# Expert gate and up rows laid over the partitions in pairs instead of in eights, in a one-core transformer and mixture-of-experts kernel

## The chip, the cores and the metric

The kernel runs on one NeuronCore of a Trainium2 chip. The metric is the device time of one execution in microseconds (us). TensorE multiplies, VectorE (DVE), ScalarE (ACT) and GpSimd (POOL) do the elementwise work, and SyncE (SP) issues every DMA of this kernel on one queue, which 16 DMA engines serve. All data is float32.

## The reference, cut to what matters

Two attention layers come first; they keep their code in this change. Behind the third, small attention layer stands a mixture of experts for 256 tokens of width 1024:

```python
# 32 experts, each token goes to a few of them
logits = h @ router_w                     # choose experts, weights wt[t, e]
for e in range(32):
    g = h @ gate_w[e]                     # gate_w[e]: 1024 x 512
    u = h @ up_w[e]                       # up_w[e]:   1024 x 512
    out += wt[:, e] * ((silu(g) * u) @ down_w[e])   # down_w[e]: 512 x 1024
```

gate_w, up_w and down_w are 2 MB (2,097,152 bytes) for each expert, 201 MB for all 32, and every expert's weights are read once. The contraction of g and u runs over the 1024 rows of gate_w[e] and up_w[e]; in which order the rows are taken doesn't matter, as long as the tokens' columns are taken in the same order.

## The kernel before

Weights travel through six buffers `ring0` to `ring5` of 128 partitions x 4096 elements (2 MB each), in the order of a list `chunks` in the front part (about 50 chunks of 2 KB runs for the most part), and by hand-written lines for the experts. `load_expert(j, e)` (L455) issues one load of 2 MB: j = 0, 1, 2 are gate, up and down of an even expert, 3, 4, 5 those of an odd one. Each load waits first until the ring buffer is free: `load_gathered` waits on the semaphore `g_gu` (a gate and up product is done) or `g_down` (a down product is done). The gate weights of experts 2, 6, 10, ... go to a seventh home, `probs` (`load_third_gate`, L461). Weights of experts 0 to 3 are loaded ahead, those of experts 2 and 3 partly in pieces into tiles that have become free (`load_third_up`, L466, into MOD; `load_fourth_up`, L471, into seven small homes; the gate of expert 3 into Y and hT). What is left when the first `g_gu` arrives is gate and up of experts 4 to 31 (28 + 28 loads) and down of experts 3 to 31 (29 loads, the last one in two halves): 85 loads of 2 MB.

The experts are taken in 8 quads of 4. A quad's tokens are gathered by matrix products: `gather(q, half)` (L2398) has a 128-column slice of the tokens' rows Y as the stationary operand and the selection matrix SEL (128 columns, 32 slots for each of four experts) as the moving one, so that XG gets the transposed tokens of four experts. Since a matmul in float32 is two instructions on TensorE, a half is 4 x 2 x 2 = 16 of them. Slice k of the contraction holds the rows 8p + k of the weights (p is the partition), so it is read as

```python
Y[:, t, 4 * half + k:D:KD]      # every eighth element, KD = 8
```

`gather_first(t)` (L2492) is the same for quad 0, taken in two steps t as soon as the tokens of 128 rows have chosen their experts. Ahead of the second step stand `place_second` (L2388, L2389, waits for the choice `mk` of the second 128 tokens) and one residual product (L2330). `gate_up(q, s)` (L2413) computes gate and up of one expert in 64 instructions of 32 stationary columns and 256 moving ones; `turn_hidden` (L2443) turns the hidden rows, with the stationary operand `HID[:, j:256:2]`, every second element; `down` (L2461) is the down product, `add_outputs` (L2478) adds four experts' outputs to the residual in PSUM.

TensorE's order inside a quad is written out by hand: for s = 0 to 3 gate_up, then for s = 0 the outputs of the quad before, for s = 1 and 2 one half of the gather of the next quad, then turn_hidden and down. The gather runs 14 times as a half (quads 1 to 7) and twice as gather_first. ACT copies the gathered tokens from PSUM (L917 for the first quad's first half), DVE the second half (L1762).

Before the quads SP, TensorE, DVE and ACT each read a flag (`crowd`, L1759) and branch: with at most 32 tokens for each expert they take the quads, and otherwise a dense path, which the data of this case doesn't take.

Of the kernel before, what the change touches and what calls it, by code (L numbers as in the profile page):

```python
# [8 lines left out]
P = 128  # L9
D = 1024  # L10
SEQ = 256
NT = SEQ // P
KD = D // P
# [7 lines left out]
FC = 4  # L21
# [66 lines left out]
def build(nc, x, ab_w, ab_out_w, cd_w, cmp_w1, cmp_w2, uq_w, ukv_w, cd_out_w, ada_w, ada_b, in_w, pool_mt, pool_w,  # L88
# [4 lines left out]
    with ctx:  # L93
        def sb(name, shape, dt=F32):
            return ctx.enter_context(nc.sbuf_tensor(name, shape, dt))
# [24 lines left out]
        def upto(name, n):  # L120

            return sem(name), before_stage.get(name, 0) + n

        def sem(name):
            name = stage_of.get(name, name)
            if name not in made:
                made[name] = ctx.enter_context(nc.semaphore("s_" + name))
            return made[name]


        ring = [sb(f"ring{i}", [P, SLOT]) for i in range(SLOTS)]
        X = sb("X", [P, NT, D])
        hT = sb("hT", [P, KD, SEQ])
        Y = sb("Y", [P, NT, AB_N])
        MOD = sb("MOD", [P, 6, D])
        QT = sb("QT", [P, 16, SEQ])
        probs = sb("probs", [P, SLOT])
        PB = probs[:, 0:2048].rearrange("p (a n) -> p a n", a=2)
        PTB = probs[:, 2048:4096].rearrange("p (a b n) -> p a b n", a=2, b=2)
        C = sb("C", [P, CO["cos64"][0] + 1024])  # L140
# [26 lines left out]
        bank = [banks[:, i, :] for i in range(8)]  # L167
# [6 lines left out]
        chunk0 = sb("chunk0", [P, 512])  # L174


        def const(name, rows=P):
            a, n = CO[name]
            return C[0:rows, a:a + n]
# [5 lines left out]
        ident = const("ident")  # L185
# [50 lines left out]
        def spare(a):  # L236
            return Y[:, 0, 2048 + a:2304 + a].rearrange("p (t n) -> p t n", t=NT)

        SEL, SW, SWT = spare(0), spare(256), spare(512)
# [4 lines left out]
        def rows(w, k):  # L244
            return w.rearrange("(p k) n -> p k n", k=k)
# [24 lines left out]
        half, first = KD // 2 * AB_WIDTHS[0], rows(ab_w, KD)[:, :, 0:AB_WIDTHS[0]]  # L270
# [49 lines left out]
        def eslot(j):  # L320

            return (E0 + j) % SLOTS

        hT_flat = hT[:, :, :].rearrange("p k n -> p (k n)")
# [61 lines left out]
        def gathered_landed(eng, q, s, j):  # L386
# [15 lines left out]
            if (e, j) in ahead:  # L402
# [2 lines left out]
            eng.wait_ge(*upto(f"slot{slot}", loads_of[slot] + 16 * (e // 2 + 1)))  # L405

        dead, late = CO["cos64"][0], KD + D
        up3_homes = [(0, 1, chunk0[:, :]), (1, 2, C[:, dead:dead + 1024]), (3, 1, Y[:, 1, 2048:2560]),
                     (4, 1, SMB[:, late:late + 512]), (5, 1, latent[:, 0:512]), (6, 1, soft[:, :]), (7, 1, tmp[:, :])]

        block = ctx.enter_context(nc.Block())
# [9 lines left out]
        def _(sp):  # L421
# [7 lines left out]
            off, n, k, src = first_rows  # L429
            sp.dma_start(ring[0][:, off:off + n].rearrange("p (k n) -> p k n", k=k), src).then_inc(sem("ld_first"), 16)  # L430
            for i, (name, parts, _) in enumerate(chunks):
# [4 lines left out]
                if i >= SLOTS:  # L436
                    s, n = chunks[i - SLOTS][2]
                    sp.wait_ge(*upto(s, n))
                for off, n, k, src in parts:
                    dst = ring[i % SLOTS][:, off:off + n].rearrange("p (k n) -> p k n", k=k)  # L440
# [7 lines left out]
                if name == "win0":  # L448
                    sp.wait_ge(*upto("pv", U0[3]))
                    sp.dma_start(mod_flat[:, 5120:6144], ada_b[:, 5120:6144]).then_inc(sem("ld_b"), 16)  # L450
            srcs = [lambda e: gate_w[bass.ds(e, 1), :, :].rearrange("e (p k) f -> p (e k) f", k=KD),
                    lambda e: up_w[bass.ds(e, 1), :, :].rearrange("e (p k) f -> p (e k) f", k=KD),
                    lambda e: down_w[bass.ds(e, 1), :, :].rearrange("e (p c) n -> p (e c) n", c=FC)]

            def load_expert(j, e):  # L455
                k = KD if j % 3 < 2 else FC
                sp.dma_start(ring[eslot(j)][:, :].rearrange("p (k n) -> p k n", k=k), srcs[j % 3](e))\
                  .then_inc(sem(f"slot{eslot(j)}"), 16)

            def load_third_gate(e):  # L460
                sp.dma_start(probs[:, :].rearrange("p (k n) -> p k n", k=KD), srcs[0](e)).then_inc(sem("ahead0"), 16)  # L461

            gate3, up2, up3, down2 = srcs[0](3), srcs[1](2), srcs[1](3), srcs[2](2)

            def load_third_up(row):
                sp.dma_start(MOD[:, row, :].rearrange("p (k n) -> p k n", k=2), up2[:, 2 * row - 2:2 * row, :])\  # L466
                  .then_inc(sem("ahead1"), 16)

            def load_fourth_up(homes):
                for at, n, dst in homes:  # L470
                    sp.dma_start(dst.rearrange("p (k n) -> p k n", k=n), up3[:, at:at + n, :]).then_inc(sem("ahead4"), 16)  # L471

            def load_first(j):
                s, n = chunks[NFRONT - SLOTS + j][2]
                sp.wait_ge(*upto(s, n))
                load_expert(j, j // 3)
# [10 lines left out]
            sp.wait_ge(*upto("pT", U0[4]))  # L487
            sp.wait_ge(*upto("pv", U0[4]))
            load_third_gate(2)
            sp.dma_start(Y[:, :, D:2 * D].rearrange("p t (k n) -> p t k n", k=2),  # L490
                         gate3[:, 4:8, :].rearrange("p (t k) n -> p t k n", t=2)).then_inc(sem("ahead3"), 16)
            load_first(3)
            sp.wait_ge(*upto("esub", 2))
            sp.dma_start(SMB[:, KD:KD + D].unsqueeze(1), down2[:, 2:3, :]).then_inc(sem("ahead2"), 16)
# [7 lines left out]
            sp.wait_ge(*upto("moe_xn", NT))  # L502
            load_third_up(3)
            sp.wait_ge(*upto("route_mm", NT))
            sp.dma_start(hT_flat.rearrange("p (k n) -> p k n", k=4), gate3[:, 0:4, :]).then_inc(sem("ahead3"), 16)
            sp.wait_ge(*upto("x_in", 2))
            sp.dma_start(X[:, :, :], down2[:, 0:2, :]).then_inc(sem("ahead2"), 16)

# [20 lines left out]
            def load_gathered(j, e, freed_by):  # L529

                sp.wait_ge(*upto("g_down" if j % 3 == 2 else "g_gu", freed_by + 1))
                if e % 4 == 2 and j % 3 == 0:
                    load_third_gate(e)
                else:
                    load_expert(j, e)
# [1271 lines left out]
        def _(pe):  # L1807
# [240 lines left out]
            for t in range(NT):  # L2048
                K = P * (t + 1)
                for h in range(4):  # L2050
                    r = slice(64 * (h % 2), 64 * (h % 2) + 64)
                    ins = pe.matmul(bank[(2, 6)[t] + h % 2][:, (h // 2) * SEQ:(h // 2) * SEQ + K],
                                    QT[r, 10 + h // 2, t * P:(t + 1) * P], QT[r, 12, 0:K], start=True, stop=True)
# [66 lines left out]
            for l in range(0, 32, 2):  # L2120
                half = l // 16
                for odd in range(2):
                    for i in range(2):
                        r, o = slice(64 * i, 64 * i + 64), 64 * i + 32 * odd
                        ins = pe.matmul(bank[5][o:o + 32, 0:128], cin[half][r, :, l % 16 + odd],
                                        w1[r, l + odd, :], start=(l == 0), stop=(l == 30))
# [56 lines left out]
            for t in range(NT):  # L2183
                for r in range(4):
                    ins = pe.matmul(bank[6 + t][:, 32 * r:32 * r + 32], QT[:, r, t * P:(t + 1) * P],
                                    kcT[:, :, :].rearrange("p g n -> p (g n)"), start=True, stop=True)
# [199 lines left out]
            def place_second():  # L2386
                pe.wait_ge(*upto("mk", 2))
                pe.matmul(bank[2][:, NE:2 * NE], before, MK[:, 1, :], start=False, stop=False)  # L2388
                pe.matmul(bank[2][:, 2 * NE:3 * NE], ones, MK[:, 1, :], start=False, stop=True).then_inc(sem("place"), 1)  # L2389

            def gather(q, half):

                pe.wait_ge(*upto("g_sel", q + 2))
                if half == 0:
                    pe.wait_ge(*upto("g_swc", q))
                for k in range(4):
                    for t in range(NT):
                        ins = pe.matmul(bank[3 * half][:, P * k:P * k + P], Y[:, t, 4 * half + k:D:KD], SEL[:, t, :],  # L2398
                                        start=(t == 0), stop=(t == NT - 1))
                ins.then_inc(sem("g_x"), 1)  # L2400

# [83 lines left out]
            def gather_first(t):  # L2485

                pe.wait_ge(*upto("g_sel", t + 1))
                for half in range(2):
                    if t == 0 and half == 1:
                        pe.wait_ge(*upto("logits", 2))  # L2490
                    for k in range(4):
                        ins = pe.matmul(bank[3 * half][:, P * k:P * k + P], Y[:, t, 4 * half + k:D:KD], SEL[:, t, :],  # L2492
                                        start=(t == 0 and k == 0), stop=(t == NT - 1 and k == 3))
                    if t == NT - 1:
                        ins.then_inc(sem("g_x"), 1)
# [32 lines left out]
            with pe.Else():  # L2528
                pe.wait_ge(*upto("g_xc", 1))
                pe.wait_ge(*upto("g_xv", 1))  # L2530
                for b in range(4, 8):

                    pe.matmul(bank[b][:, :], identb[:, :], zerob[:, :], start=False, stop=True).then_inc(sem("x_closed"), 1)
                for t in range(NT):
                    for half in range(2):
                        if t > 0:
                            pe.wait_ge(*upto("h_back", half + 1))
                        for k in range(4):
                            ins = pe.transpose(bank[half][:, k * P:(k + 1) * P], Y[:, t, 4 * half + k:D:KD], ident)
                        ins.then_inc(sem("h_again"), 1)  # L2540
                pe.wait_ge(*upto("h_back", 4))
                pe.wait_ge(*upto("x_back", 4))
                expert(0, 0, 0, True)
                expert(1, 1, 0, False)
                expert(2, 0, 1, False)
                expert(3, 1, 1, False)
                with pe.Fori(2, NE // 2) as i:
                    for s in range(2):
                        expert(i * 2 + s, s, i, False)
# [98 lines left out]
```

## Time and profile before

| what | value |
|---|---|
| time, median of 3 runs | 909.06 us (908.38, 909.06, 916.39) |
| span of the profiled execution | 909.3 us |
| its own time | not listed apart from the three runs; the span is 0.2 us above their median |
| TensorE busy (matmul) | 775.5 us, 85% |
| DVE, ACT, POOL busy | 41%, 19%, 4% |
| read from HBM | 282.75 MB |
| mean granted TensorE clock | 0.949 of full speed |

The span is what the first to the last instruction take. Busy time of matmuls is modelled, so a busy TensorE is not one at its peak. In a DMA row "packets" are the single transfers that the 16 engines made, one for each unbroken run of a partition and one of a few bytes for each completion, of which a DMA makes 16; "under 512 B" counts the completions in most windows, and the counts under 2 KB and under 8 KB contain the smaller ones.

### The profile page before, as it was taken

What the parts mean: (1) busy time and instruction counts of PE and PEld (TensorE: products, weight loads), DVE (VectorE), ACT (ScalarE), POOL (GpSimd) and SP (SyncE); (2) the same over time, 40 slices, a digit from 0 to 9 for tenths busy, and PEclk for the clock granted to TensorE, in tenths of its full rate; (3) what the DMA queues carried; (4) which work ended last, traced back from release to release, by engine and by line L of the source; (5) the groups of instructions that cost most, each with busy time, mean ns of one, the idle gap of its engine ahead of it and who ended that gap; (6) DMA issues with size and microseconds to landing.
All of it is one profiled execution on the core that took longest, in us unless ns stands there. A gap on an engine that the chain in (4) does not pass through costs nothing.

```text
span 909.3 us, 13058 instructions
## 1 busy us (share of the span) xinstructions
PE 775.5 (85%) x5393; PEld 465.6 (51%) x5393; DVE 373.5 (41%) x885; ACT 168.4 (19%) x473; POOL 40.5 (4%) x36
## 2 busy tenths in 40 slices
PE   7999899999998999999999987858766686677655
PEld 3544664456476644456578573535534444344332
DVE  2478668557854676766441212111111111121113
ACT  3222630223356301041120100000010100001001
POOL 1110000012400000001000000000000000000000
PEclk9999999999999999999999997889899889899888
DMA  9984506765002749987679999999999999999994
GB/s 343 394 291 155 186 1 241 269 231 186 1 1 82 277 130 352 392 338 321 232 269 396 406 425 430 430 430 427 426 427 429 430 428 429 427 428 429 427 428 162
DMA packets 54555, 284.38 MB, mean 313 GB/s; under 512 B 2800, under 2 KB 7280, under 8 KB 41968
## 3 DMA queue, kind: packets, MB, share of 16 engines
q1 hardware_dynamic: 54512, 283.81, 78.0%
q8 instruction: 27, 0.44, 0.2%
q14 instruction: 16, 0.13, 0.0%
HBM read 282.75 MB, written 1.05 MB: 312 GB/s over the span
## 4 chain that ended last, share of the span: by engine, by line
PE 55%; DMA 34%; DVE 5%; issue 2%; ACT 2%; POOL 1%; SPq 1%; DVEq 0%; POOLq 0%
DMA ring<-in_up_w 30%; PE banks L2002 15%; PE banks L1850 9%; PE banks L2413 8%; PE banks L2248 4%; DMA ring<-in_down_w 3%; PE banks L1954 3%; PE banks L2461 2%; PE banks L1882 2%; PE banks L2398 2%; DMA ring<-in_ada_w 1%; PE banks L1929 1%; POOL rs L590 1%; PE banks L1980 1%; PE banks L2492 1%
## 5 line engine op out<-in xcount | busy, mean ns | idle before, releaser
L2413 PE MATMUL banks<-ring,QT 128*32 128x256 f32 x1696 | 143.0, 445 | 56.7 <-DMA ring<-in_up_w 56.7
L2002 PE MATMUL banks<-ring,hT 128*128 128x512 f32 (+4 forms) x384 | 157.9, 566 | 2.4 <-DMA ring<-in_ab_w 2.1
L2413 PEld LDWEIGHTS banks<-ring,QT 128*32 128x32 f32 x1696 | 71.9, 123 | 105.7 <-DMA ring<-in_up_w 44.1
L2002 PEld LDWEIGHTS banks<-ring,hT 128*128 128x128 f32 x384 | 72.4, 193 | 75.5 <-issue 68.6
L1746 DVE TENSOR_TENSOR QT<-banks,MOD 32x256 f32<-32x256 f32 x128 | 53.8, 421 | 138.5 <-PE banks L2461 137.2
L1737 DVE TENSOR_TENSOR QT<-QT,banks 64x256 f32<-64x256 f32 x32 | 13.5, 423 | 191.4 <-ACT QT L943 191.4
L1850 PE MATMUL banks<-ring,hT 128*128 128x512 f32 x192 | 83.9, 594 | 1.9 <-ACT hT L628 1.8
L2461 PE MATMUL banks<-ring,QT 128*32 128x256 f32 x992 | 66.0, 408 | 14.6 <-ACT QT L950 12.4
L590 POOL TENSOR_TENSOR rs<-st,mhalf 128x1 f32<-128x1 f32 (+7 forms) x27 | 33.3, 1237 | 863.3 <-DVE st L1783 451.7
L943 ACT ACTIVATE QT<-banks 64x256 f32<-64x256 f32 x32 | 12.0, 375 | 294.4 <-PE banks L2413 294.4
L1185 DVE SCALAR_TENSOR_TENSOR extra<-ring,cs,extra 128x512 f32<-128x512 f32 x84 | 63.1, 752 | 2.9
L2413 PE MATMUL banks<-probs,QT 128*32 128x256 f32 x256 | 41.6, 492 | 25.1 <-DMA ring<-in_up_w 25.1
L1850 PEld LDWEIGHTS banks<-ring,hT 128*128 128x128 f32 x192 | 36.0, 190 | 46.9 <-issue 43.1
L2398 PEld LDWEIGHTS banks<-Y 128*128 128x128 f32 x224 | 54.4, 334 | 6.1 <-issue 6.1
L2398 PE MATMUL banks<-Y 128*128 128x128 f32 x224 | 57.1, 408 | 0.0
L2248 PE MATMUL banks<-ring,hT 128*128 128x512 f32 x128 | 56.5, 596 | 0.2 <-DVE MOD L1193 0.2
L2461 PEld LDWEIGHTS banks<-ring,QT 128*32 128x32 f32 x992 | 37.1, 114 | 31.2 <-issue 18.7
L664 ACT ACTIVATE probs<-banks,soft 128x256 f32<-128x256 f32 (+1 forms) x96 | 39.9, 432 | 32.9 <-DVE soft L1104 31.1
L2413 PEld LDWEIGHTS banks<-probs,QT 128*32 128x32 f32 x256 | 21.0, 136 | 42.6 <-issue 38.9
L2248 PEld LDWEIGHTS banks<-ring,hT 128*128 128x128 f32 x128 | 23.8, 190 | 30.9 <-issue 28.4
L2478 PE MATMUL banks<-QT,Y 128*128 128x512 f32 x64 | 31.2, 632 | 1.9 <-DVE QT L1746 1.9
L1094 DVE TENSOR_REDUCE soft<-banks 128x4 f32<-128x1024 f32 (+1 forms) x24 | 24.0, 1002 | 16.7 <-PE banks L1893 15.1
(361 smaller groups left out, 767.6 us busy)
## 6 DMA issues: line engine op xcount, KB each, us to landing
ring<-in_down_w SPq DMA_DIRECT2D x30, 2048.0 KB, 21.8
ring<-in_up_w SPq DMA_DIRECT2D x30, 2048.0 KB, 23.6
ring<-in_gate_w SPq DMA_DIRECT2D x23, 2048.0 KB, 20.4
ring<-in_ada_w SPq DMA_DIRECT2D x12, 2048.0 KB, 15.4
probs<-in_gate_w SPq DMA_DIRECT2D x8, 2048.0 KB, 29.2
ring<-in_ab_w SPq DMA_DIRECT2D x4, 2048.0 KB, 19.4
ring<-in_cd_w SPq DMA_DIRECT2D x4, 2048.0 KB, 13.5
ring<-in_in_w SPq DMA_DIRECT2D x4, 2048.0 KB, 14.5
```

The costliest lines, as they stand in the source:

```text
L590: pool.tensor_tensor(rs[0:r, a:a + k], st2[0:r, a:a + k], mhalf[0:r, a:a + k], ALU.pow)\
L664: act.activation(PB[:, u % 2, h * K:(h + 1) * K], score_of(u, h), ACT.Exp, bias=nmx[:, 4 * u + h:4 * u + h + 1], scale=scale, accum_out=sm ...
L1185: ins = v.scalar_tensor_tensor(out=acc, in0=w[:, k, :], scalar=by, in1=acc, op0=ALU.mult, op1=ALU.add)
L1746: ins = v.tensor_tensor(YE[CAP * s:CAP * s + CAP, 256 * c:256 * c + 256], bank[2][CAP * c:CAP * c + CAP, 0:256], MOD[CAP * s:CAP * s + CAP ...
L1850: ins = pe.matmul(bank[j % 4][:, 0:n], hT[:, k, t * P:(t + 1) * P], w[:, k, :], start=(k == 0), stop=(k == KD - 1))
L1954: ins = pe.matmul(value_bank(u)[:, P * h:P * h + v.shape[1]], PTB[:, u % 2, kb, h * P:(h + 1) * P], v, start=(kb == 0), stop=(kb == nb - 1))
L2002: ins = pe.matmul(bank[b][:, 0:n], hT[:, k, t * P:(t + 1) * P], w[:, k, :], start=(k == 0), stop=(k == KD - 1))
L2248: ins = pe.matmul(win_bank(c, t)[:, :], hT[:, k, t * P:(t + 1) * P], w[:, k, :], start=(k == 0), stop=(k == KD - 1))
L2398: ins = pe.matmul(bank[3 * half][:, P * k:P * k + P], Y[:, t, 4 * half + k:D:KD], SEL[:, t, :], start=(t == 0), stop=(t == NT - 1))
L2413: return pe.matmul(bank[1][CAP * j:CAP * j + CAP, 0:256], XG[:, k, CAP * s:CAP * s + CAP], wk[:, :, 2 * (j % 2):2 * (j % 2) + 2], start=(k ...
L2461: ins = pe.matmul(bank[2][CAP * n:CAP * n + CAP, 0:256], HG[:, a:a + CAP], wd(c)[:, 256 * n:256 * n + 256], start=(c == 0), stop=(c == FC ...
L2478: ins = pe.matmul(bank[4 + j][:, :], SWT[:, j // 2, :], YE[:, 512 * (j % 2):512 * (j % 2) + 512], start=False, stop=last)
```

## The change

Row r of an expert's gate and up weights sat on partition r // 8 at place r % 8. Now it sits in block r // 256, on partition (r % 256) // 2, at place r % 2: each partition holds two consecutive rows of each block of 256. The gather reads its slices accordingly, with a step of 2 in place of 8. down_w keeps its layout. The homes of expert 3's up weights are rearranged (which slice goes to which small tile), with the same number of pieces and bytes.

```diff
-        up3_homes = [(0, 1, chunk0[:, :]), (1, 2, C[:, dead:dead + 1024]), (3, 1, Y[:, 1, 2048:2560]),
+        up3_homes = [(2, 1, chunk0[:, :]), (0, 2, C[:, dead:dead + 1024]), (3, 1, Y[:, 1, 2048:2560]),
...
-            srcs = [lambda e: gate_w[bass.ds(e, 1), :, :].rearrange("e (p k) f -> p (e k) f", k=KD),
-                    lambda e: up_w[bass.ds(e, 1), :, :].rearrange("e (p k) f -> p (e k) f", k=KD),
+            def paired_rows(w):
+                return lambda e: w[bass.ds(e, 1), :, :].rearrange("e (j p i) f -> p (e j) (i f)", p=P, i=2)
+
+            srcs = [paired_rows(gate_w), paired_rows(up_w),
                     lambda e: down_w[bass.ds(e, 1), :, :].rearrange("e (p c) n -> p (e c) n", c=FC)]
 
             def load_expert(j, e):
-                k = KD if j % 3 < 2 else FC
-                sp.dma_start(ring[eslot(j)][:, :].rearrange("p (k n) -> p k n", k=k), srcs[j % 3](e))\
+                sp.dma_start(ring[eslot(j)][:, :].rearrange("p (k n) -> p k n", k=4), srcs[j % 3](e))\
                   .then_inc(sem(f"slot{eslot(j)}"), 16)
 
             def load_third_gate(e):
-                sp.dma_start(probs[:, :].rearrange("p (k n) -> p k n", k=KD), srcs[0](e)).then_inc(sem("ahead0"), 16)
+                sp.dma_start(probs[:, :].rearrange("p (k n) -> p k n", k=4), srcs[0](e)).then_inc(sem("ahead0"), 16)
...
             def load_third_up(row):
-                sp.dma_start(MOD[:, row, :].rearrange("p (k n) -> p k n", k=2), up2[:, 2 * row - 2:2 * row, :])\
+                sp.dma_start(MOD[:, row, :].unsqueeze(1), up2[:, row - 1:row, :])\
                   .then_inc(sem("ahead1"), 16)
 
             def load_fourth_up(homes):
                 for at, n, dst in homes:
-                    sp.dma_start(dst.rearrange("p (k n) -> p k n", k=n), up3[:, at:at + n, :]).then_inc(sem("ahead4"), 16)
+                    a = 512 * (at % 2)
+                    sp.dma_start(dst.unsqueeze(1), up3[:, at // 2:at // 2 + 1, a:a + 512 * n]).then_inc(sem("ahead4"), 16)
...
-            sp.dma_start(Y[:, :, D:2 * D].rearrange("p t (k n) -> p t k n", k=2),
-                         gate3[:, 4:8, :].rearrange("p (t k) n -> p t k n", t=2)).then_inc(sem("ahead3"), 16)
+            sp.dma_start(Y[:, :, D:2 * D], gate3[:, 2:4, :]).then_inc(sem("ahead3"), 16)
...
-            sp.dma_start(hT_flat.rearrange("p (k n) -> p k n", k=4), gate3[:, 0:4, :]).then_inc(sem("ahead3"), 16)
+            sp.dma_start(hT_flat.rearrange("p (k n) -> p k n", k=2), gate3[:, 0:2, :]).then_inc(sem("ahead3"), 16)
...
+            def expert_rows(t, k):
+                a = 2 * P * (k // 2) + k % 2
+                return Y[:, t, a:a + 2 * P:2]
+
...
-                        ins = pe.matmul(bank[3 * half][:, P * k:P * k + P], Y[:, t, 4 * half + k:D:KD], SEL[:, t, :],
+                        ins = pe.matmul(bank[3 * half][:, P * k:P * k + P], expert_rows(t, 4 * half + k), SEL[:, t, :],
```

The last replacement stands in gather, in gather_first and in the dense path. No instruction, wait, DMA or semaphore is added or removed on any engine.

## Rows read from the trace of the kernel before

**Rows 1.** The page: 40 equal slices of the span (22.7 us each).

```profile
PE   7999899999998999999999987858766686677655
DMA  9984506765002749987679999999999999999994
GB/s 343 394 291 155 186 1 241 269 231 186 1 1 82 277 130 352 392 338 321 232 269 396 406 425 430 430 430 427 426 427 429 430 428 429 427 428 429 427 428 162
```

**Rows 2.** The chain that ended last, in order of time: start us, us, what.

```profile
458.60 3.89 PE banks L2492 x16
...
463.80 3.82 PE banks L2492 x16
467.62 3.84 PE banks L2413 x62
...
543.73 23.32 DMA ring<-in_up_w
...
835.75 24.94 DMA ring<-in_up_w
```

**Rows 3.** Waits of TensorE, 545 to 880 us: us in total, times, longest.

```profile
PE banks L2413 <- DMA ring<-in_up_w: 81.9, 23, 6.9
```

**Rows 4.** SP's queue in order of time: start us, us, the load issued.

```profile
471.48 0.34 SPq L457 DMA_DIRECT2D ring<-in_gate_w  x1
...
571.35 0.43 SPq L457 DMA_DIRECT2D ring<-in_up_w  x1
...
806.27 0.43 SPq L457 DMA_DIRECT2D ring<-in_up_w  x1
```

**Rows 5.** The page, DMA issues: count, KB each, median us to landing.

```profile
ring<-in_up_w SPq DMA_DIRECT2D x30, 2048.0 KB, 23.6
```

**Rows 6.** DMA traffic, 550 to 860 us (expert loads alone).

```profile
DMA packets 9117, 132.78 MB, mean 428 GB/s; under 512 B 1012, under 2 KB 1012, under 8 KB 1012
```

**Rows 7.** DMA traffic, 350 to 370 us (runs of 2 KB).

```profile
DMA packets 3865, 7.81 MB, mean 390 GB/s; under 512 B 59, under 2 KB 59, under 8 KB 3864
```

**Rows 8.** DMA traffic, 425 to 426 us (Y<-in_gate_w, runs of 4 KB).

```profile
DMA packets 101, 0.42 MB, mean 422 GB/s; under 512 B 1, under 2 KB 1, under 8 KB 100
```

**Rows 9.** DMA traffic, 303.5 to 305.5 us (two of 512 KB, runs of 4 KB).

```profile
DMA packets 229, 0.80 MB, mean 400 GB/s; under 512 B 22, under 2 KB 22, under 8 KB 228
```

**Rows 10.** DMA traffic, 455.5 to 459.5 us (MOD<-in_up_w, runs of 4 KB).

```profile
DMA packets 344, 1.38 MB, mean 346 GB/s; under 512 B 43, under 2 KB 43, under 8 KB 331
```

**Rows 11.** Instructions of single lines: duration ns min/median/max, first and last start.

```profile
L2398 PEld LDWEIGHTS banks<-Y x224: 312/336/338, 479.0 to 825.3; 128*128 128x128 f32 x112
L2443 PEld LDWEIGHTS banks<-C,QT x128: 189/193/193, 472.4 to 892.3; 64*128 64x128 f32 x128
L1954 PEld LDWEIGHTS banks<-Y,probs x192: 186/192/193, 97.8 to 284.3; 128*128 128x128 f32 x192
```

**Rows 12.** The chain in order of time, gather and attention products: start us, us, what.

```profile
279.35 1.73 PE banks L1954 x16
...
521.98 4.01 PE banks L2398 x16
```

**Rows 13.** Timeline around the two steps of gather_first.

```profile
460.16 0.18 DVE L1647 TENSOR_SCALAR MK<-rt 128x32 f32<-128x32 f32 x1
...
462.20 0.32 PEld L2388 LDWEIGHTS banks<-MK,C 128*128 128x128 f32 x2
...
463.61 0.15 DVE L1759 TENSOR_SCALAR crowd<-st 128x1 int32<-128x1 f32 x1
...
465.74 0.60 ACT L917 ACTIVATE QT<-banks 128x512 f32<-128x512 f32 x1 [9.93 <-PE banks L2492]
```

**Rows 14.** DMA traffic, 486 to 494 us and 508 to 528 us.

```profile
DMA packets 184, 2.68 MB, mean 335 GB/s; under 512 B 20, under 2 KB 20, under 8 KB 20
...
DMA packets 550, 7.98 MB, mean 399 GB/s; under 512 B 63, under 2 KB 63, under 8 KB 63
```

**Rows 15.** Timeline, the last down product and the first output norm.

```profile
893.93 2.14 PE L2461 MATMUL banks<-ring,QT 128*32 128x256 f32 x32 [1.28 <-DVE QT L1746]
```

More of the change, by code:

```diff
@@ L2491, in gather_first @@
                     for k in range(4):
-                        ins = pe.matmul(bank[3 * half][:, P * k:P * k + P], Y[:, t, 4 * half + k:D:KD], SEL[:, t, :],
+                        ins = pe.matmul(bank[3 * half][:, P * k:P * k + P], expert_rows(t, 4 * half + k), SEL[:, t, :],
                                         start=(t == 0 and k == 0), stop=(t == NT - 1 and k == 3))
@@ L2538, in _ @@
                         for k in range(4):
-                            ins = pe.transpose(bank[half][:, k * P:(k + 1) * P], Y[:, t, 4 * half + k:D:KD], ident)
+                            ins = pe.transpose(bank[half][:, k * P:(k + 1) * P], expert_rows(t, 4 * half + k), ident)
                         ins.then_inc(sem("h_again"), 1)
```

## The prediction

> **What bounds the kernel now.** I read four views, in this order. The page's slices [rows 1] show two kernels in one: up to slice 20 (455 us) TensorE is busy and the DMA engines often are not; from slice 23 on the DMA engines are at 9 tenths and move 425 to 431 GB/s in every slice, while TensorE drops to 5 to 7 tenths. The chain that ended last [rows 2] agrees: up to 543 us it consists almost wholly of TensorE work, from there of a dozen pieces of 23 to 25 us that are DMAs of up_w or down_w, each followed by one 3.8 us gate_up. The waits say it again: TensorE waits 23 times for up_w, 81.9 us in all [rows 3]. SP's queue gives the depth: a load of up_w lands 23.6 us after its issue in the median [rows 5]. Between 571.35 and 806.27 us the weights of 16 experts, 48 loads, are issued [rows 4], so a load takes 234.92 / 48 = 4.894 us, and 4.5 to 5 loads are always queued. From 545 us the stage is a queue of bytes: neither an engine nor a wait for a buffer matters, and the end comes when the last load has landed, plus a tail of 16 us (the last down product starts at 893.93 us [rows 15]) which holds no gather and stays.
>
> The stage before it matters through its start. The first buffer comes free at the end of expert 0's gate_up, when the first of the 85 loads left is issued (471.48 us, [rows 4]); ahead of it the chain runs through both steps of gather_first and one gate_up [rows 2]. 85 x 4.894 = 416.0 us of pure transfer follow.
>
> **What the change does, part by part.**
>
> *Shorter runs, on the path.* Which runs do the loads consist of? From 550 to 860 us there are 9117 - 1012 = 8105 data packets for 132.78 MB, 16.4 KB each [rows 6]: today a partition's eight rows are one run of 16 KB. After the change a partition has four runs of 4 KB for gate and up; down keeps 16 KB. A run's time is 16 engines by the window over its runs. 16 KB: 16 x 310 / 8105 = 612.0 ns [rows 6]. 2 KB: 16 x 20 / (3865 - 59) = 84.1 ns [rows 7]. A straight line between them has a fixed part of 8.7 ns for each run and gives 84.1 + 527.9 x 2048 / 14336 = 159.5 ns for 4 KB. The trace has 4 KB runs only in short stretches. One in the middle of a 1 MB transfer: 99 data runs of 4 KB and one of 16 KB in 1 us, (16 - 0.6) / 99 = 155.5 ns [rows 8]. One with two DMAs of 512 KB: 206 runs for 0.80 MB, so some 185 of 4 KB and 21 of 2 KB, (32 - 1.8) / 185 = 163.4 ns [rows 9]. I take the line, which lies between them and rests on thousands of runs. A load of 8 x 612.0 = 4.896 us becomes 32 x 159.5 = 5.104 us: 0.208 us more, and 56 of the 85 loads are of gate or up: **+11.6 us**. The ends: +4.5 us by rows 8 (4.976 us each), +18.6 us by rows 9 (5.229 us each). A third stretch [rows 10] is slower yet, 346 GB/s: with its 13 long runs taken off, (64 - 8.0) / 288 = 194 ns, which would be 6.2 us a load and +74 us; but it holds short DMAs of 512 KB and 43 completions, and I don't take it as an end, only as the reason for a tail above the range.
>
> The Trainium skill, page "DMA: Bandwidth & Descriptors", section "Specifications", asks for at least 512 B in a transfer for the full line rate, by which 4 KB and 16 KB would be the same and this part would cost nothing. Rows 6 and 7 speak against it: 2 KB runs, four times that size, move 390 GB/s with the engines just as full as at 428.
>
> *Loads ahead of the first experts, hidden.* The five whole gate and up loads and the pieces for experts 2 and 3 that are issued from 378 us on get the same 0.2 us each. They run in slices 16 to 19, where the DMA engines are at 6 to 8 tenths [rows 1], and those for expert 0 are issued 60 us before they are used. Cost nothing; without that cover it would be 1 us. MOD's pieces and the seven small homes keep their run lengths and counts.
>
> *SP's issue, hidden.* A load of four times as many runs may take SP longer to issue. With over four loads queued behind each other [rows 4, 5] an issue could be some microseconds late without effect.
>
> *The gather's step, beside other work for the most part.* The stationary operand with step 8 loads in 336 ns, one with step 2 (L2443) in 193 ns, and one with step 1 (L1954) in 192 ns [rows 11]. So step 2 is as cheap as none. 16 instructions of the gather take 4.01 us, 16 of the attention product, of the same 128 x 128 x 128 shape, 1.73 us [rows 12]: 2.3 us less for each half. In the DMA-bound stretch that only lengthens TensorE's waits. Two places count.
>
> First, gather_first, ahead of the first free buffer. Its first step starts at 458.60 us on the chain and would end near 460.4. `place_second` starts at 462.20 us today, behind it; DVE had the choice `mk` of the second tokens ready at 460.34 [rows 13], so place_second could start near 460.6, 1.6 us earlier, the dependent DVE operations follow along, and the second step is 2.1 us shorter (3.82 [rows 2] to 1.73): 3.7 us. What is late next? ACT's copy of the first half has to be done before gate_up; with the second step at 1.7 us that copy of 0.6 us [rows 13] starts 0.9 us before the step's end, which is just enough. The flag is the other candidate: it is written at 463.76 [rows 13], and TensorE must read it and branch ahead of gate_up at 467.6. Today 3.9 us cover that, then 1.8 us. What the branch takes the trace doesn't show; between nothing and the whole 3.7 us can be lost. I take nothing, since no gap behind it is seen today. **-3.7 us** (0 to -3.8).
>
> Second, the holes in the DMA stream between 471 and 545 us, where TensorE is still the slower one. From 486 to 494 us 2.68 MB are moved where 8 us at 428.3 GB/s would be 3.43: 1.7 us lost. From 508 to 528 us 7.98 MB instead of 8.57: 1.4 us [rows 14]. The first hole is the wait for expert 1's down product; that comes 3.7 + 2.3 us earlier against the old clock, while the queue ahead of it, partly of longer loads, empties later relative to its start. The second follows from the same lead, now of two halves. Both go: **-3.1 us** (0 to -3.1).
>
> **The sum** against the profiled span: 909.3 + 11.6 - 3.7 - 3.1 = 914.1 us. The span is 0.2 us above the median of the runs, so the forecast is 913.9, rounded to 914.
>
> **The rivals.**
>
> A, the length of the run costs nothing. Only the gains stay: 909.1 - 6.8 = 902.3, or 907 with the 155.5 ns of rows 8. For it: one clean microsecond at 422 GB/s. Against it: the 2 KB rows, with the DMA engines just as full. 12 in 100.
>
> B, on the slower side: the 4 KB runs are dearer than the line. The four runs of one partition now lie 512 KB apart in HBM, where one engine today reads 16 KB on end and goes to the next 16 KB; each jump would cost something that a straight line through in-order runs doesn't hold. At rows 9's 163.4 ns it is 909.1 + 18.6 - 6.8 = 920.9; it decides for slower by over 1% from 161.9 ns on (+15.9 us), merely 2.4 ns above the line. For it: rows 9 and 10. Against it: the 2 KB loads of the front part also step over whole rows of a wide matrix and are the line's lower point. 18 in 100, 918 to 930. The Trainium skill's page "DMA: Bandwidth & Descriptors", section "Latency and other measured facts", has a table of row pitches in which 512 KiB moves 207 GB/s where the full rate is 214, 3% less; as an estimate from that page, 3% of 5.1 us over 56 loads would add 9 us. No row here shows such a pitch.
>
> C, the gather's gain doesn't arrive: the branch takes its place ahead of the first gate_up, or the stationary load with 128 partitions and step 2 is slower than the 64-partition one of L2443. Then 917.6 (start alone lost) to 920.7. 10 in 100.
>
> **How the numbers follow.** The forecast case (157 to 162 ns a run, both gains) covers 910 to 918 and has 55 in 100; 5 are left for what I don't see. The range of 905 to 922 holds it, the upper half of A, most of B and all of C. A change of 1% is 9.1 us, about what this measurement can tell from no change (its three runs lie 0.9% apart). Slower by over 1%: B, half of C and the rest's share, 0.26. Faster by over 1% would need more than the 6.8 us of both gains: 0.03. Within 1%: 0.71.
>
> **What the profile after would show.** Right: data packets from 550 to 860 us of 4 KB and 16 KB, 5.5 KB on average, at about 416 GB/s with full engines; a distance of some 60.4 us between corresponding loads of up_w where it is 58.7 now; L2398 and L2492 stationary loads near 192 ns; the first g_gu load issued near 467.8 us; no holes behind it. Wrong: a rate still at 428 (A), below 410 (B), or a first load still at 470 to 471 us (C). Most of what could upset the sum is a few nanoseconds in a 4 KB run, since each one is worth 1.8 us.

## The result and the profile after

The changed kernel takes 917.35 us in the median of five runs (916.62 to 917.90), the kernel before 909.06 us: a ratio of 1.009 with a 95% interval of 1.0072 to 1.0109. It is slower by 0.9%, inside the stated range of 905 to 922 and 3.4 us above the forecast of 914. The profiled execution has a span of 915.5 us against 909.3 us. The two differences (8.3 and 6.2 us) are not the same because an execution's time is longer than its span: 917.35 us stand beside 915.5, and the other four runs have the same 1.7 to 1.9 us. With that the execution profiled of the kernel before must have taken about 911 us, one of the slower ones. (Runs of the kernel before beside the later experiments have medians of 909.24 and 908.62 us, and the ratios of the experiments are against these.) A run more than 1.5% above the fastest of its kernel is left out of medians and ratios; that is one run, of 1437.46 us, of the kernel with short runs in the old order below.

The page of the kernel after, its slices of 22.9 us, answers to [rows 1]:

```profile
PE   7999899999998999999999848575776576766764
DMA  9983507665003559988689999999999999999993
GB/s 342 395 303 136 184 1 269 238 230 184 1 1 137 221 165 381 393 322 320 249 338 412 415 418 413 419 413 418 412 418 414 418 414 418 414 417 415 415 416 140
```

The front half is much as it was. From slice 23 on (counted from 0) the DMA engines are as full as before, and what they move has fallen from 425 to 430 GB/s to 412 to 419. The traffic from 550 to 860 us, then from 350 to 370 us, from 486 to 494 and from 508 to 528 us (packets, MB, rate), answers to [rows 6, 7, 14]:

```profile
DMA packets 24731, 128.76 MB, mean 415 GB/s; under 512 B 982, under 2 KB 982, under 8 KB 22168
...
DMA packets 3847, 7.77 MB, mean 388 GB/s; under 512 B 61, under 2 KB 61, under 8 KB 3846
...
DMA packets 640, 3.21 MB, mean 401 GB/s; under 512 B 30, under 2 KB 30, under 8 KB 582
...
DMA packets 1626, 8.17 MB, mean 408 GB/s; under 512 B 64, under 2 KB 64, under 8 KB 1482
```

In the first of these lines 24731 - 22168 = 2563 packets are runs of 16 KB (down) and 22168 - 982 = 21186 are runs of 4 KB. 16 engines for 310 us are 4960 us; less 2563 x 0.612 us, 3391 us are left for the short runs: 160.1 ns each. The 2 KB loads of the front, in the second line, are where they were (390 GB/s before). By the same prices the third and fourth line hold 123.9 of 128 and 315.1 of 320 us of engine time, so that some 0.3 us each are lost in the places of the two holes, where it was 1.7 and 1.4 us.

The gather's two lines, durations in ns (min/median/max), answer to [rows 11]; they were L2398 and L2492:

```profile
L2403 PEld LDWEIGHTS banks<-Y x224: 193/197/198, 473.9 to 825.6; 128*128 128x128 f32 x112
...
L2497 PEld LDWEIGHTS banks<-Y x32: 194/197/198, 457.1 to 462.2; 128*128 128x128 f32 x32
```

And the timeline from the first step of gather_first to the first load that a g_gu releases, as in [rows 2, 4, 13] (start us, us, what):

```profile
457.18 2.13 PE L2497 MATMUL banks<-Y 128*128 128x128 f32 x16
...
459.14 0.40 PE L2389 MATMUL banks<-MK,C 128*128 128x32 f32 x2
...
460.54 2.05 PE L2497 MATMUL banks<-Y 128*128 128x128 f32 x16
...
462.51 3.84 PE L2418 MATMUL banks<-ring,QT 128*32 128x256 f32 x64
...
466.41 0.38 SPq L458 DMA_DIRECT2D ring<-in_gate_w  x1
```

In the kernel before gather_first started at 458.44 us:

```profile
458.44 4.05 PE L2492 MATMUL banks<-Y 128*128 128x128 f32 x16
```

From the start of gather_first to that load it is 9.23 us; it was 471.48 - 458.44 = 13.04 us. gate_up starts right behind the second step, so neither ACT's copy nor the branch shows. But the stream of loads that starts earlier ends later. The end of the timeline has the last two down products and the outputs ([rows 15] was the last down product before):

```profile
895.67 2.52 PE L2466 MATMUL banks<-ring,QT 128*32 128x256 f32 x32 [2.54 <-DMA ring<-in_down_w]
898.12 1.11 PE L2448 MATMUL banks<-C,QT 64*128 64x64 f32 x4
900.06 3.64 PE L2466 MATMUL banks<-ring,QT 128*32 128x256 f32 x32 [0.83 <-ACT QT L951]
905.64 3.67 PE L2483 MATMUL banks<-QT,Y 128*128 128x512 f32 x8 [1.94 <-DVE QT L1747]
```

From the first load to the last down product it is 900.06 - 466.41 = 433.65 us, where it was 893.93 - 471.48 = 422.45 us. I call this the length of the stream below. What follows it, 15.4 us in both kernels, is unchanged.

### The profile page after: what moved, and what is told of

Read it like the earlier page. It is cut to its first block, busy times and chain, and to the rows that moved or that the text cites. A ratio compares the mean times of both kernels' runs of the same rounds, so it can differ in the third digit from the quotient of the medians.

```text
span 915.5 us, 13058 instructions
## 1 busy us (share of the span) xinstructions
PE 759.3 (83%) x5393; PEld 438.1 (48%) x5393; DVE 373.4 (41%) x885; ACT 168.4 (18%) x473; POOL 40.5 (4%) x36
## 4 chain that ended last, share of the span: by engine, by line
PE 56%; DMA 35%; DVE 4%; ACT 2%; issue 1%; POOL 1%; SPq 1%; DVEq 0%; POOLq 0%
DMA ring<-in_up_w 32%; PE banks L2003 15%; PE banks L2418 9%; PE banks L1851 9%; PE banks L2249 6%; DMA ring<-in_down_w 3%; PE banks L1955 2%; PE banks L1883 2%; PE banks L2466 2%; PE banks L1981 1%; PE banks L1930 1%; PE banks L1829 1%; POOL rs L591 1%; DVE soft L1095 1%; ACT probs L665 1%
## 5 line engine op out<-in xcount | busy, mean ns | idle before, releaser
L2418 PE MATMUL banks<-ring,QT 128*32 128x256 f32 x1696 | 156.8, 483 | 67.5 <-DMA ring<-in_up_w 67.5
L2418 PEld LDWEIGHTS banks<-ring,QT 128*32 128x32 f32 x1696 | 77.3, 134 | 125.0 <-issue 67.0
L2466 PE MATMUL banks<-ring,QT 128*32 128x256 f32 x992 | 69.6, 427 | 16.6 <-ACT QT L951 13.2
L591 POOL TENSOR_TENSOR rs<-st,mhalf 128x1 f32<-128x1 f32 (+7 forms) x27 | 33.3, 1237 | 869.3 <-DVE st L1784 459.0
L2466 PEld LDWEIGHTS banks<-ring,QT 128*32 128x32 f32 x992 | 38.1, 119 | 35.1 <-issue 21.6
L2403 PEld LDWEIGHTS banks<-Y 128*128 128x128 f32 x224 | 27.5, 197 | 6.1 <-issue 6.1
L2403 PE MATMUL banks<-Y 128*128 128x128 f32 x224 | 30.2, 288 | 0.0
```

The source lines that it names most:

```text
L591: pool.tensor_tensor(rs[0:r, a:a + k], st2[0:r, a:a + k], mhalf[0:r, a:a + k], ALU.pow)\
L2403: ins = pe.matmul(bank[3 * half][:, P * k:P * k + P], expert_rows(t, 4 * half + k), SEL[:, t, :], start=(t == 0), stop=(t == NT - 1))
L2418: return pe.matmul(bank[1][CAP * j:CAP * j + CAP, 0:256], XG[:, k, CAP * s:CAP * s + CAP], wk[:, :, 2 * (j % 2):2 * (j % 2) + 2], start=(k ...
L2466: ins = pe.matmul(bank[2][CAP * n:CAP * n + CAP, 0:256], HG[:, a:a + CAP], wd(c)[:, 256 * n:256 * n + 256], start=(c == 0), stop=(c == FC ...
```

## The experiments

The questions: what does a run cost by itself; is it the length of the run or the place in HBM; what is the cheaper gather worth by itself, and through what; and is there a layout that has the one without the other. In all of them the DMAs carry the same bytes. The table comes after the single experiments.

**The gather alone.**

```diff
-    Y[:, t, 4 * half + k:D:KD], SEL[:, t, :],
+    Y[:, t, 256 * (k // 2 + 2 * half) + k % 2:256 * (k // 2 + 2 * half) + 256:2], SEL[:, t, :],
```

> The kernel before (runs of 16 KB), with the gather's stationary operand read in step 2 as in the changed kernel; the weights' rows keep their old places, so the tokens' columns and the weights' rows no longer belong together: the output is not the reference's, the instructions are as many. My theory (the gather's gain is worth the start of the DMA stream and the holes behind it): 902 to 903 us, stationary loads of 192 to 197 ns, first load behind g_gu some 3.8 us earlier against the start of gather_first, and a rate of 428 GB/s from 550 us on. Rival (the branch or ACT takes over, or the holes stay): 905 to 909 us.

903.18 us, ratio 0.9933 (0.9915 to 0.9951). The rate from 550 us on is the old one, and from 470 to 550 us the holes are gone:

```profile
DMA packets 9116, 132.80 MB, mean 428 GB/s; under 512 B 1010, under 2 KB 1010, under 8 KB 1010
...
DMA packets 2340, 34.14 MB, mean 427 GB/s; under 512 B 256, under 2 KB 256, under 8 KB 256
```

Without the longer loads the change would have been a gain of 6 us. The theory holds, the rival (905 to 909 us) falls. The first load behind g_gu comes 9.27 us after the start of gather_first (9.23 us in the changed kernel).

**The runs alone.** The reverse: the changed kernel, with `Y[:, t, 4 * half + k:D:KD]` again in gather and gather_first.

> The changed kernel (runs of 4 KB), with the gather's step put back to 8 (the output is not the reference's). My theory (a 4 KB run costs 160 ns in place of 153): the DMA stream as in the changed kernel, 415 GB/s, and the first load 3.8 us later; the holes between 471 and 545 us are partly filled because the loads are longer: 919 to 923 us. Rival (the gather is worth nothing beside longer loads): 917.4, as the changed kernel.

920.61 us, ratio 1.0122 (1.0105 to 1.0139), 416 GB/s. The cost of the shorter runs is 11.4 us, and the gather gives back 920.61 - 917.35 = 3.3 us of it, not 6. The first load is 13.04 us behind the start of gather_first here, so the start gains its 3.8 us as ever; but the stream is as long without the faster gather as with it, 433.70 and 433.65 us. The traffic from 508 to 528 us shows that the longer loads have not filled the holes by themselves:

```profile
DMA packets 1188, 7.75 MB, mean 387 GB/s; under 512 B 61, under 2 KB 61, under 8 KB 933
```

These are 872 short and 255 long runs, 295.7 of 320 us of engine time: 1.5 us are lost, as in the kernel before, and 0.3 us in the changed kernel. The first hole, from 486 to 494 us, is nearly gone without the gather (0.3 us lost). What hides the gather's second gain is in part the clock: up to the second to last down product the stream takes 429.88 us here and 429.26 us in the changed kernel, and only then the changed kernel's products run slower, by 0.6 us (see the last section). Why these 0.6 us are not the whole 1.2 us of the second hole I haven't followed.

**Short runs in the old HBM order.**

```diff
+            def swapped(w):
+                return lambda e: w[bass.ds(e, 1), :, :].rearrange("e (p b i) f -> p (e b) (i f)", b=4, i=2)
...
+                    sp.dma_start(ring[eslot(j)][:, :].rearrange("p (k n) -> p k n", k=4)[:, ::-1, :], whole[j % 3](e))\
```

> The kernel before with its rows where they were, but each partition's 16 KB of gate and up are written to SBUF in four pieces of 4 KB whose order is reversed (and read accordingly by TensorE), so that a run is 4 KB long while HBM is read in the old order, without jumps of 512 KB; the gather has step 8; output as the reference. If the length of the run is the cost: 415 GB/s and the same time as the kernel with short runs and step 8, 919 to 923 us. If the jump in HBM is the cost: 428 GB/s and 909 us, as before.

921.38 us in the median, ratio 1.0129 (1.0107 to 1.0152), and the traffic from 550 to 860 us:

```profile
DMA packets 24394, 128.85 MB, mean 416 GB/s; under 512 B 985, under 2 KB 985, under 8 KB 21710
```

The same rate, packets and length of the stream (434.35 us) as with jumps of 512 KB. So it is the number of runs that costs, not where in HBM the next one lies: rival B's mechanism is refuted. Source and destination are both cut into 4 KB here and in the changed kernel; which side of the transfer pays for a run was not parted.

**Tokens written in the order of the slices.** The layout of the weights is the old one; the order is changed on the other side, where VectorE writes Y.

```diff
+                    if tag == "wout":
+                        by_slice = Y[:, t, 0:D].rearrange("p (k n) -> p n k", k=KD)[:, 64 * c:64 * c + 64, :]
+                        link(v.tensor_tensor(by_slice, X[:, t, cols].rearrange("p (n k) -> p n k", k=KD),
+                                             MOD[:, scale, cols].rearrange("p (n k) -> p n k", k=KD), ALU.mult), tag + "_y")
...
+                                          in1=MOD[:, 3, :].rearrange("p (n k) -> p k n", k=KD), op0=ALU.mult, op1=ALU.add),
```

> The kernel before with runs of 16 KB, and the tokens' rows Y written by VectorE in the order of the slices (the scaling of X and the last norm read and write with a step), so that the gather and the transposes read 128 consecutive elements; output as the reference. My theory: as with step 2 and old runs, 901 to 904 us, if VectorE's steps cost nothing; each of its five operations that gets a step is 0.7 to 1.3 us long and near the path, so up to 4 us more if a step makes them twice as long. Rival (the step on VectorE eats the gain): 906 to 909 us.

904.97 us, ratio 0.9947 (0.9929 to 0.9965). VectorE's two operations, grouped (line, operation, shapes and count | busy us, mean ns of one | idle before), first of the kernel before, then of this one:

```profile
L1043 DVE TENSOR_TENSOR Y<-X,MOD 128x512 f32<-128x512 f32 x4 | 2.8, 691 | 0.1
L1629 DVE SCALAR_TENSOR_TENSOR Y<-Y,rs,MOD 128x1024 f32<-128x1024 f32 x2 | 2.6, 1285 | 1.3 <-POOL rs L590 1.3
```

```profile
L1045 DVE TENSOR_TENSOR Y<-X,MOD 128x512 f32<-128x512 f32 x4 | 4.2, 1062 | 0.1
L1634 DVE SCALAR_TENSOR_TENSOR Y<-Y,rs,MOD 128x1024 f32<-128x1024 f32 x2 | 4.1, 2072 | 1.3 <-POOL rs L590 1.3
```

The steps make them 1.5 and 1.6 times as long, 0.4 us and 0.8 us each, and the last ones stand ahead of the routing. gather_first starts at 459.04 us, the latest of all kernels run. Most of the gain survives. Some 1.3 to 1.8 us don't, against the next version and the gather alone; the intervals of the three ratios overlap, and that VectorE's steps are the cause is likely but not shown. The time lies between the two cases expected.

**The weights laid out ahead of the launch.**

```diff
+    def by_slice(w):
+        return w.reshape(NE, KD, P, 512).transpose(0, 2, 1, 3).reshape(NE, D, 512)
...
+        "gate_w": by_slice(a["w_gate_2"][0]), "up_w": by_slice(a["w_up_2"][0]), ...
```

> The kernel before, with the rows of gate_w and up_w put in another order when the inputs are laid out ahead of the launch (partition p holds rows 128k + p at place k), so that a partition's 16 KB stay one run and the gather reads 128 consecutive elements of Y; output as the reference. Nothing on VectorE changes. My theory: the gather's gain alone, as with step 2 and old runs, 902 to 903.5 us. If a step of 1 were cheaper than a step of 2 (192 against 197 ns a load), it would be within 0.5 us of that.

903.71 us, ratio 0.9939 (0.9918 to 0.9960), 428 GB/s and 16 KB runs, 0.2 us above what was expected. This version beats both kernels, and no engine does more for it; it leans on the weights being stored in another row order, as the kernel's layout step already does with the columns of the attention weights.

**The first gather alone.** The edit of the gather alone, in gather_first only.

> The kernel before (runs of 16 KB), with step 2 in the two steps of gather_first alone and step 8 in the 14 halves of the quads (the output is not the reference's). It parts the gain of the gather alone (6.1 us) into the earlier start and the filled holes: my theory is 3.8 us for the start, with the holes left for the most part, 905 to 906 us. Rival (an earlier start is lost again in holes as long as TensorE is the slower): 907 to 909 us.

904.59 us, ratio 0.9951 (0.9934 to 0.9967), below both expected cases. The gather's whole gain is 6.1 us (903.18), and 4.0 to 4.7 us of it come from the first two steps (against 908.62 and 909.24 us). The length of the stream is 421.06 us, against 420.33 us with the whole gather and 422.45 us before; more than half of the holes' 2.1 us is gone with the early start alone. I had expected them to stay. Differences below a microsecond between single profiles are at the edge of what I trust, so the split between start and holes is only rough.

**Runs of 8 KB, step 4.** `paired_rows` with i=4 in place of i=2, and the slices' step 4.

> Four consecutive rows of each block of 512 on a partition: runs of 8 KB for gate and up, gather with step 4; output as the reference. The straight line gives 310 ns for a run of 8 KB, a load of 4.965 us, 3.9 us more than before for 56 loads. If the stationary load with step 4 costs 193 to 197 ns like step 2: 906 to 907 us. If step 4 costs as much as step 8 (336 ns): 912 to 914 us, and so in between for a load in between.

912.41 us, ratio 1.0036 (1.0020 to 1.0051): the second case. The stationary loads, grouped (mean ns after the comma):

```profile
L2414 PEld LDWEIGHTS banks<-Y 128*128 128x128 f32 x224 | 53.4, 328 | 6.1 <-issue 6.1
```

**Runs of 2 KB, step 1.** i=1; expert 3's gate half for Y takes two DMAs in place of one.

> One row of each block of 128 on a partition: runs of 2 KB for gate and up, gather with step 1; output as the reference. A constant cost for each run gives 64 x 84.1 ns = 5.38 us a load, 27.2 us more for 56 loads, less 6 us for the gather: 929 to 932 us, at about 400 GB/s from 550 us on (two thirds of the loads short). If shorter runs hid part of their cost at this length: under 925 us.

934.86 us, ratio 1.0270 (1.0240 to 1.0299), above the 929 to 932 us expected. The length of the stream is 450.17 us, 29.8 us longer than with the gather alone: that is the whole expectation of the runs (27.2) and 2.6 us more. A run took 84.8 ns (worked out below the table) where 84.1 were expected, and 56 loads of 64 runs make 2.5 us of that. gather_first starts at 458.96 us here, 1.5 us later than there; whether the longer loads ahead of it cause that I haven't followed.

```profile
DMA packets 43693, 123.88 MB, mean 400 GB/s; under 512 B 950, under 2 KB 950, under 8 KB 41158
...
L2416 PEld LDWEIGHTS banks<-Y 128*128 128x128 f32 x224 | 26.1, 191 | 6.0 <-issue 6.0
```

The table, in us; "stream" is from the first load behind g_gu to the last down product in the profile, "run" is a run of gate and up worked out as above from the packets of 550 to 860 us, "load" the stationary load of the gather:

| kernel | median | run, bytes | run, ns | step | load, ns | stream |
|---|---|---|---|---|---|---|
| before | 909.06 | 16384 | 612.0 | 8 | 334 | 422.45 |
| gather alone | 903.18 | 16384 | 612 | 2 | 197 | 420.33 |
| weights laid out | 903.71 | 16384 | 612 | 1 | 191 | 420.09 |
| runs of 8 KB | 912.41 | 8192 | 311.0 | 4 | 328 | 425.38 |
| runs alone | 920.61 | 4096 | 160 | 8 | 334 | 433.70 |
| after | 917.35 | 4096 | 160.1 | 2 | 197 | 433.65 |
| runs of 2 KB | 934.86 | 2048 | 84.8 | 1 | 191 | 450.17 |

For 8 KB: 14384 - 1000 = 13384 runs with 131.35 MB are 10734 of 8 KB and 2650 of 16 KB; (4960 - 2650 x 0.612) / 10734 = 311.0 ns. For 2 KB: (4960 - 2535 x 0.612) / 40208 = 84.8 ns. A line through the ends, 84.8 and 612.0 ns, gives 160.1 and 310.7 ns in between, and 9.5 ns for a run of no length. The cost is a constant for each run.

## Why the prediction was right, and where it was off

**The bound** was read rightly: a queue of bytes that ends 15.4 us before the span does. The gather cut 1.9 us of TensorE's time from every half, and behind 550 us, where the queue never ran empty, nothing came of it.

**The runs.** 159.5 ns were forecast by the straight line, 160.1 ns measured; 32 x 160.1 = 5.123 us a load, 0.227 us more, 12.7 us for 56 loads in place of 11.6. This is the term behind the sign. The choice between the line and the two short stretches of [rows 8, 9] was right, and the stretch of [rows 10] was indeed no measure of a load.

**The gather.** 193 ns a load were forecast from the turned hidden rows, 197 measured, and 2.08 us for a half where I had taken 1.73; on the path from gather_first to the first load 3.7 us were forecast and 3.8 came. What I left open, the branch and ACT's copy, cost nothing.

**The holes.** The term was -3.1 us, and its size was off: with long runs the gather makes the stream 2.1 us shorter, not 3.1, so the sum was mis-sized by 1.0 us. Its reason holds: "The second follows from the same lead, now of two halves". With longer loads and the old gather the first hole all but closes, the second stays at 1.5 us, and it goes with the gather's lead. Since the longer loads close one hole by themselves, the runs' and the gather's effects overlap and don't add: 11.4 alone and -6.1 alone give 5.3, together they are 8.3. By the prices of a run the DMA engines lose, in the 80 us behind the first load, 4.5 us before, 3.3 with the runs alone, 1.8 with the gather alone and 1.7 in the changed kernel; 1.1 us of the 3 us of overlap are thus the hole that both close. Another 0.6 us is the clock in the last products, and the rest is not traced.

**The sum.** In spans the forecast was 914.1 us and 915.5 came: +1.1 for the runs, +1.0 for the holes, -1.3 because gather_first starts earlier in this profile (457.18 against 458.44 us, ahead of anything that the gather does; from 456.4 to 459.0 us over all kernels, without an edit ahead of it in most), and +0.6 us for a slower clock in the last products, below. The remaining 2 us up to the median's 917.35 come from the step that carried the span over to the runs: "The span is 0.2 us above the median of the runs". It compared a span with times that hold 1.85 us more than their spans.

**The rivals.** A is refuted by the rate; B's threshold of 161.9 ns was missed by 1.8 ns, and its mechanism, the jump, does nothing measurable: a run of 4 KB takes 160.1 ns with jumps and without. The 3% of the Trainium skill's page "DMA: Bandwidth & Descriptors", section "Latency and other measured facts", doesn't show here; its pitch of 512 KiB is from one partition to the next in copies between HBM tensors, while here the 512 KB lie between the runs of one partition. C is refuted for the start, where all of the gain arrives. The time alone couldn't tell, since 917.35 us lie inside the forecast case (910 to 918) and 0.25 us below C's 917.6; the first load at 466.41 us does. The time is in the upper end of that case by the sum of small terms and not by another mechanism. The Trainium skill's page "DMA: Bandwidth & Descriptors", section "Specifications", by whose 512 B the layout would have cost nothing, is not borne out: with two thirds of the bytes in runs of 4 KB the rate is 415 in place of 428 GB/s, 3% less.

## What to carry to other kernels

Where a stage lives on DMA alone, the layout in HBM is to be chosen by the length of a partition's unbroken run first: on this queue each run costs some 9.5 ns beside its bytes, 1.5% of the time at 16 KB, 6% at 4 KB, 11% at 2 KB. A faster engine beside such a stage is worth only what it does to the first transfer and to holes in the stream, so an edit that speeds up an engine and shortens runs is to be split and timed in halves; here the good half (0.6 to 0.7%) was hidden in a change that lost 0.9%. Before a step is bought with shorter runs, look whether the order can be changed on the other side, in how the data is stored or in the write of the small operand.

## What the runs showed of the hardware that I had not expected

The stationary load's price does not fall evenly with the step. 128 columns of float32 take 191 ns with step 1, 197 with 2, 328 with 4 and 334 with 8. The Trainium skill, page "SBUF — State Buffer", section "Specifications (TRN2)", says that SBUF has lines of 16 bytes and that full bandwidth needs two hits in a line. The trace agrees: steps 1 and 2 have four and two elements in 16 bytes, steps 4 and 8 have one.

SyncE was held up at many issues once the loads had more runs, up to 8 us for one load, where from 490 us on no load in the kernel before took more than 1.2 us. The longest were loads of down_w, whose own runs are as few as before, so that the length of a load's own list doesn't explain them. It cost nothing, since the DMA engines stayed full (from 625 to 640 us 415 GB/s, as in the whole stage):

```profile
630.82 7.96 SPq L458 DMA_DIRECT2D ring<-in_down_w  x1
```

The end of the kernel depends on TensorE's clock at the last products. The windows of the kernel after (us, busy PE, PEld, DVE, ACT and POOL with counts, granted clock, DMA share, GB/s):

```profile
885.00:895.00 10.00, 7.31 (x68) 4.16 (x68) 0.85 (x2) 0.96 (x3) 0.00 (x0) 1.00 1.02 421
895.00:900.00 5.00, 3.56 (x36) 1.95 (x36) 1.69 (x4) 0.28 (x1) 0.00 (x0) 0.69 0.56 234
900.00:905.00 5.00, 3.64 (x32) 1.59 (x32) 1.21 (x3) 0.00 (x0) 0.00 (x0) 0.63 0.00 0
905.00:910.00 5.00, 3.67 (x8) 1.44 (x8) 1.46 (x5) 2.71 (x8) 0.55 (x1) 1.00 0.01 3
```

TensorE had waited 2.54 us for the second to last down weights at 895.67 us, and then the clock was granted at 0.69 and 0.63, means of stretches at 2.4 and at 1.2 GHz. The two down products took 2.52 and 3.64 us, and 1.93 and 2.15 us in the kernel with the gather alone, where the clock was 1.00 from 880 to 890 us. The kernel before had its slow stretch at the outputs (5.31 us in place of 3.67), so the tails came out alike; such pieces of 0.6 to 1.6 us are part of why single profiles differ by a microsecond or two.
